# Sub keys kept in their first place for both tiles, and a row buffer that joins the ring later

## The reference

```python
q = (xf @ w_pq).reshape(n_tok, P_HEADS, 2, P_DHALF)
s = jnp.einsum('thpd,phkd->thpk', q, sub_keys)          # scores against the sub keys
top_s, top_i = lax.top_k(s, P_TOPK)
...                                                      # 16 x 16 candidates, top 16: idx, gate
u = expert_u[it]                                         # 128 experts for each token
h = jax.nn.gelu(jnp.einsum('td,tkd->tk', xt, u), approximate=False)
v = expert_v[it]
return jnp.einsum('tk,tkd->td', gt * h, v)
```

## Time and profile before

| | |
|---|---|
| time, median of 3 runs | 1735.94 us (1735.91 to 1737.31) |
| the profiled execution's own time | 1734.31 us |
| its span, first to last instruction | 1732.5 us |
| what lies around the span | 1.8 us |
| mean granted TensorE clock | 0.967 |
| PE, DVE, ACT, POOL busy | 91%, 55%, 26%, 18% |
| bytes moved by DMA | 465 MB |
| of these by the rows (POOL's queue) | 268 MB |

### The profile page before, as it was taken

How to read it: one execution, slowest core, us unless ns; L and a number is a source line. 1 busy time by engine, 2 the same in 40 slices (tenths; PEclk the granted TensorE clock), 3 DMA queues, 4 the chain that set the end, 5 groups by cost and what they waited for, 6 DMA issues and landing times.

```text
span 1732.5 us, 20909 instructions
## 1 busy us (share of the span) xinstructions
PE 1569.6 (91%) x8432; PEld 1029.1 (59%) x8432; DVE 957.2 (55%) x1864; ACT 446.8 (26%) x1034; POOL 313.0 (18%) x271
## 2 busy tenths in 40 slices
PE   8999999999989979879598766789999999999998
PEld 7867555558455444446244222249996486599953
DVE  3343443216788653588976566544756415366654
ACT  1143352102346441233343222221000023210001
POOL 0000000002134433334465444400000000000000
PEclk9999999999999999999789988999999999999999
DMA  6364222257999999999999999994443423354432
GB/s 236 139 233 156 99 98 98 98 194 294 424 404 420 423 414 418 421 421 416 421 421 421 421 422 421 422 389 166 150 182 142 191 118 112 138 213 165 177 146 97
DMA packets 54490, 465.21 MB, mean 269 GB/s; under 512 B 6645, under 2 KB 8053, under 8 KB 9850
## 3 DMA queue, kind: packets, MB, share of 16 engines
q0 software_dynamic: 36864, 268.45, 37.3%
q1 hardware_dynamic: 17530, 195.43, 29.6%
HBM read 462.81 MB, written 1.05 MB: 268 GB/s over the span
## 4 chain that ended last, share of the span: by engine, by line
PE 71%; DMA 17%; DVE 7%; issue 2%; ACT 2%; POOL 1%; SPq 0%; DVEq 0%; POOLq 0%; ACTq 0%
DMA main<-in_expert_uv,main 14%; PE ps L2479 14%; PE ps L956 10%; PE ps L439 7%; PE ps L2421 7%; PE ps L395 6%; PE ps L2633 6%; DMA panels<-in_wall 3%; PE ps L2399 3%; PE ps L220 3%; PE ps L435 2%; PE ps L2708 2%; PE ps L2393 2%; DVE main L884 1%; PE ps L1222 1%
## 5 line engine op out<-in xcount | busy, mean ns | idle before, releaser
L956 PE MATMUL ps<-main 128*128 128x512 f32 x724 | 348.9, 631 | 103.9 <-ACT main L931 103.7
L866 POOL DMA_INDIRECT main<-in_expert_uv,main x208 | 248.5, 1195 | 383.3 <-PE ps L956 244.5
L956 PEld LDWEIGHTS ps<-main 128*128 128x128 f32 x724 | 140.8, 202 | 293.7 <-issue 150.3
L884 DVE SCALAR_TENSOR_TENSOR main<-main 128x1024 f32<-128x1024 f32 x208 | 249.1, 1222 | 113.3 <-DMA main<-in_expert_uv,main 112.2
L2421 PE MATMUL ps<-xT,panels 128*128 128x256 f32 x576 | 127.3, 383 | 1.6 <-DMA panels<-in_wall 1.6
L2421 PEld LDWEIGHTS ps<-xT,panels 128*128 128x128 f32 x576 | 110.0, 192 | 17.5 <-DMA panels<-in_wall 1.8
L395 PE MATMUL ps<-panels,xT 128*128 128x512 f32 x256 | 113.6, 597 | 0.0
L919 ACT ACTIVATE main<-main 128x2 f32<-128x2 f32 x128 | 25.8, 202 | 323.9 <-DVE main L884 275.2
L2479 PE MATMUL ps<-main 128*128 128x128 f32 x912 | 104.9, 275 | 0.0
L2479 PEld LDWEIGHTS ps<-main 128*128 128x128 f32 x912 | 103.4, 192 | 0.0
L956 PE MATMUL ps<-panels,main 128*128 128x512 f32 x160 | 80.2, 647 | 13.4 <-ACT main L931 13.4
(11 more groups left out here) (345 smaller groups left out, 2180.2 us busy)
## 6 DMA issues: line engine op xcount, KB each, us to landing
panels<-in_wall SPq DMA_DIRECT2D x85, 2048.0 KB, 8.0
main<-in_rows SPq DMA_DIRECT2D x8, 512.0 KB, 9.7
main<-in_expert_uv,main POOLq DMA_INDIRECT x208, 18.1
main<-in_sub_keys SPq DMA_DIRECT2D x2, 1024.0 KB, 12.9
panels<-in_wall SPq DMA_DIRECT2D x2, 1024.0 KB, 4.9
main<-in_wall SPq DMA_DIRECT2D x1, 2048.0 KB, 9.5
x<-in_x SPq DMA_DIRECT2D x2, 512.0 KB, 3.8
main<-in_pool_w SPq DMA_DIRECT2D x1, 1024.0 KB, 29.6
```

The source lines that it names most:

```text
L866: pool.indirect_dma_start(out=self.bufs[self.buf_of[r]], out_offset=None, in_=self.c.dram["expert_uv"], in_offset=bass.IndirectOffsetOnAxi ...
L884: dve.scalar_tensor_tensor(out=u, in0=u, scalar=1.0, in1=self.c.row(m, H2), op0=ALU.mult, op1=ALU.mult, accum_out=self.dots_at[:, m, q:q + ...
L956: mm = pe.matmul(self.c.ps[:, b, :], self.diags[self.of_pe(r) % DIAG_RING], v[:, half * HALF:(half + 1) * HALF], start=(q == 1), stop=(q = ...
```

## The change

The sub keys get one place for both tiles, columns 2D to 4D of `main`, and SP loads them for tile 0 only. Tile 1's scores wait for the same single load. Since the keys now lie in buffer 5's place until tile 1 has its last scores, buffer 5 joins the ring at row 152 (128 + 24) and not at row 24.

```diff
-        self.spans.update({n: [(CHOICE_FREE, end)] for n in range(4, 7)})
+        self.spans.update({4: [(CHOICE_FREE, end)], 5: [(SLOTS + CHOICE_FREE, end)], 6: [(CHOICE_FREE, end)]})
...
-        self.keys = slot(2, 2 * P_HEADS, N_KEYS)
+        self.keys = c.area(2 * D, 2 * P_HEADS, N_KEYS)
...
-            pe.wait_ge(*c.keys_loaded.count(16 * (m + 1)))
+            pe.wait_ge(*c.keys_loaded.count(16))
...
-        sp.wait_ge(c.panel_done.sem, FIRST[t.pq])
-        sp.dma_start(t.keys, c.dram["sub_keys"]).then_inc(c.keys_loaded.sem, 16)
+        if m == 0:
+            sp.wait_ge(c.panel_done.sem, FIRST[t.pq])
+            sp.dma_start(t.keys, c.dram["sub_keys"]).then_inc(c.keys_loaded.sem, 16)
```

## The result

| | before | after |
|---|---|---|
| time, median of 6 runs each, us | 1735.93 (1732.73 to 1737.31) | 1744.16 (1740.96 to 1746.94) |
| ratio, 95% interval | | 1.0050 [1.0037, 1.0062] |
| profiled execution, own time / span | 1734.31 / 1732.5 | 1743.41 / 1741.6 |
| mean granted TensorE clock | 0.967 | 0.963 |
| bytes moved by DMA, MB | 465 | 464 |

The change makes the kernel 0.5% slower: +8.7 us by the ratio, with an interval from 6.4 to 10.8. In two later jobs the same two kernels stood at 1.0057 [1.0037, 1.0077] and 1.0057 [1.0040, 1.0074]. The forecast was +1.6 us and its range ended at +6.5.

The account below looks back on a forecast made before the run. The rows' stretch was taken as bound by DMA bytes at 421 GB/s plus idle moments. Terms -2.5 + 0.4 + 1.8 + 0.8 + 1.0 + 0.3 = +1.8, less 0.2 overlap, +1.6: 1737.5 us from the median; range 1733.7 to 1742.4.

Parts of the forecast that it names:

- The end: Last rows: feed-forward panels, asked for one row sooner, can stretch row 255; 0 to 2 us, taken as 0.3.
- Rival 4: End decides: feed-forward panels take bandwidth from row 255, +2 us, 1739.2; or PE profits from them, 0; chance 0.06.
- Rows 72 and 80: Rows waiting for later releases around TensorE's blocks: row 72 costs 1.8 us, row 80 0 to 2.5, taken as 0.8.
- Row 28: Issued at 525.45, not 518.61, so it lands later than its stream slot; 0.3 to 0.8 us, taken as 0.4.
- Row 136: Waits for the release at 851.73, not 832.29, but still lands before its slot; cost nothing, 0.8 us to spare.
- Row 116: With 10 buffers it waits for row 106's sum, issued at 803.39, not 788.57; 0.7 to 1.4 us, taken as 1.0.
- Row 91: Waits for the release of 724.19; at most 1.5 of the 2.5 us survive, but backlog fills it, taken as 0.
- the keys' 2.5 us: Gain from one 1 MB key load fewer in the full DMA stretch: -2.5 us at 421 GB/s.
- Rows 56 to 58: Ring falls to 8 buffers, not 12; panels asked for sooner cover it, taken as 0, without cover about 2 us.
- Rival 1: Saved megabyte mostly comes through; only rows 91 and 116 cost: -0.8 us, or -2.5 with neither; chance 0.16.
- Rival 2: Short ring starves the stream at four PE blocks, rows 56 to 103: +8.8 us, with two +3.8; chance 0.16.
- Rival 3: Keys not safe or not at hand for tile 1, so its scores wait; price 0, no separate chance given.

Follow-up runs that it names:

- The kernel with only this piece: Kernel before, keys loaded twice, buffer 5 away only for rows 56 to 103 (eight buffers there), end as before: +4.3 us [2.3, 6.4].
- The experiment: Kernel before with buffer 5 out for rows 130 to 151, panels in the ring from row 129 so the end stays: +1.6 us [-0.5, 3.8].

## Why the prediction was wrong

The bound was read rightly: the rows' stretch ends with the last byte, and what follows the last sum did not change (569.3 and 569.5 us). The places were mostly right too. One size clearly was not, the end; rows 72 and 80 cost more than their term by the middle of the measured interval, which still holds it.

- **The end, the step that failed most.** "On the chain this can stretch the last row: 0 to 2 us, I take 0.3." It costs 4.0 us [2.1, 6.1]. Row 255's landing was stretched by 3.1 us in the traces (5.55 for 2.47 us behind row 254), more than the upper end. The second half was missing altogether: behind the longer idle time that a late dot makes on PE the granted clock falls, and the last sums take 6.63 for 3.70 us. Rival 4 had the mechanism's first half and the wrong size, +2. By the Trainium skill's page "DMA: Bandwidth & Descriptors", section "Queues, rings and completion order", each DMA engine takes turns between the queues that have work for it, a packet at a time; the trace agrees, with 129 panel packets ahead of the row's last one and not 30. The estimate of up to 2 us that the prediction hung on it was too low.
- **Rows 72 and 80.** 1.8 + 0.8 = 2.6 us were forecast for them. The kernel with only this piece measured +4.3 us [2.3, 6.4], its trace 3.3 between rows 66 and 83; the three traces of after show 2.9, 2.6 and 2.5, and the unchanged kernel's second one 2.1, so the size rests on the time. Row 72 was dear in the sum and cheap in the traces (rows 66 to 79: 0.8, 1.2 and 0.2), row 80 the reverse: 0.8 forecast, 2.1, 1.4 and 2.3 seen. The sum also read two landings wrong: a dot that waits starts 0.02 us behind its row's landing and not 0.4 or 0.5, so row 73 landed at 653.58 and row 121 at 821.22, and by the sum's own rule row 72 costs 1.4 and not 1.8 us, row 116 0.2 and not 0.7.
- **Row 28.** 0.4 forecast, 2.1, 2.1 and 1.1 in the three traces of after, and 0.1 and 0.4 in two other profiles with the same ring there. The step priced the landing at the least value of the whole trace, 5.6 us; it was 8.1, 6.0 and 7.0, and the rows behind it started 2.9 to 3.1 us apart. The same error, "issue plus 5.6", lies in every step: it was 5.7 to 8.4 us at rows 72 and 116 and 7.6 to 9.2 us at rows 80 and 91. Whether the 2 us reach the end of the kernel is not settled.
- **Row 136 and what follows.** "Nothing, with 0.8 us to spare." By first packets the traces of after lose 2.6, 2.3 and 1.9 us between rows 121 and 147: behind row 136, issued at 853.51 after 20.00 us of wait, and in the first two behind row 144, which waits 6.77 and 6.62 us where the longest such wait there was 4.41. (In the third it waits 4.24.) By landings row 136 is no later than row 121, as forecast; the loss is row 144's, which I had not looked at at all, and 1.5, 0.9 and 0.0 us of it are left at row 254. The experiment gives +1.6 [-0.5, 3.8].
- **Row 116.** 1.0 forecast, 1.2 to 1.6 seen in the traces between rows 104 and 121 (0.4 in the second one of before), and nothing that the times can tell when it was done alone.
- **Row 91 and rows 95 to 98.** "... there is backlog to fill it, and I take 0": the keys' 2.5 us came back as 1.8 to 2.2 by row 94. Of this 0.8 to 1.2 went again by row 104, which had no step in the sum.
- **Rows 56 to 58** at 0 were right: the restart's panels, asked for at 589.56 and not 598.38, covered them, and from row 31 to row 66 the lateness does not move.
- **Rival 1** is excluded. **Rival 2** had almost the total, +8.8 us, but by four stops of 2.5 us in tile 1's blocks; the traces show one such stop, at row 80, and smaller ones elsewhere. **Rival 3** cost nothing: PE's one wait of line 1654 for the keys is 0.5 us at 402.6 us, in tile 0, where it is before the change as well.

The wait by PE for the keys in after, from the list of waits (total us, times, longest):

```profile
PE ps L1654 <- DMA main<-in_sub_keys: 0.5, 1, 0.5
```

The range failed because its upper end took the sum of what each step could cost as I had listed the steps. It allowed the end 2.0 us at most, which costs 4.0 by the time and 4.7 to 6.6 in the traces. Two steps were not on the list: the clock of the last sums, which was on the chain, and row 144, of which that is not shown.

## What to carry to other kernels

In a ring that feeds a full DMA stream, a buffer less can be paid wherever a burst of releases comes late, and a stream that is full behind it gave little of the time back here (row 83 to row 254). Price such a place by the rate of rows issued just in time (2.9 to 3.1 us each at rows 28 to 31), not by the least time from issue to landing. When a ring changes length, look at where the rows next to a hand-over fall, hundreds of rows later: here the last rows in the panels moved by one, and that one row was nearly half of the loss. When the last transfer gets later, add what TensorE's clock does to the work behind it.

## What the runs showed of the hardware that I had not expected

- Eight matmul records of 128x512 took 3.70 us behind 1.2 us of idle PE in every profile with the request of before or a later one, and 5.4 to 6.6 us behind 4.3 to 5.0 us of idle in the eight with the earlier one; in the first of these the granted clock was 0.83 over 20 us. With the request after the last dot 3.2 us of idle were followed by 64 records of 128x128 that took 8.84 and not 7.31 us.
- It takes little to stretch a row: in the eight profiles in which two panels of plain DMA were asked for 3.0 us before row 254 landed, row 255 landed 5.5 to 6.2 us behind it. In the twelve with the request 1.3 us before that landing or later it was 2.4 to 2.5 us, the row's plain share of the stream.
- With rows 28 to 31 issued only 2.0 to 4.6 us before their first packets, the stream moved 359 GB/s at a DMA share of 0.96, against 419 at 1.01. I did not test why.
- In seven profiles DVE stood for 2 to 5 us in all, within the choice of tile 1's experts between the dots of rows 121 and 122 (25.2 to 28.6 us in place of 23.2 to 23.4). It delays the rows there, also with an unchanged ring (27.8 us in the kernel with the request after the last dot). Six of the seven have a single pause of 1.9 to 3.1 us that the profile puts down to no instruction of this core. These are all the profiles of two of the jobs, in which the kernel before stood at 1738.9 and 1740.3 us and not at 1734.0 to 1736.3 as in the others; the cause is open.
